# A two-block transformer kernel on one core: the blocks of the mixed branches follow the steps of the MLA's heads by a table, in place of an even spread

## What is computed

```python
proj = h @ w_in
(dn_q, dn_k, dn_v, dn_z, dn_alpha, dn_beta,
 mla_q, mla_ckv, mla_kr, gate_dn, gate_mla) = jnp.split(proj, split_at, axis=-1)
...
o_a = rms_norm(o_a, dn_norm_w) * jax.nn.silu(dn_z)          # gated output of the delta rule
y_a = o_a.reshape(B, S, DN_V) @ w_out_dn
o_b = mla_attention(mla_q, mla_ckv, mla_kr, positions, ...)   # 8 heads, 128 + 64 (rotary) columns
y_b = o_b.reshape(B, S, MLA_VD) @ w_out_mla
mix = jax.nn.sigmoid(gate_dn) * y_a + jax.nn.sigmoid(gate_mla) * y_b
x = x + gate1 * (mix @ w_o)
```

## Time and profile before

| what | value |
|---|---|
| median of 3 runs | 2372.3 us (2370.41 to 2372.65) |
| the profiled execution, time | 2371.21 us |
| its span, first to last instruction | 2369.4 us |
| mean granted TensorE clock | 0.985 of full speed |
| instructions | 26883 |
| busy: PE, DVE, ACT, POOL | 2289.3, 1117.2, 939.0, 685.2 us |
| MLA's norms and heads | about 517 to 834 |
| banded attention, gated linear attention | about 1563 to 1739, 1739 to 1845 |

### The profile page before, as it was taken

The page is one execution under the profiler, slowest core; times in us unless marked ns, Lnnn a source line. Parts: engine busy times, 40 slices in busy tenths (PEclk is TensorE's granted clock), DMA queues, the critical chain, the costliest instruction groups (busy, mean ns, idle before and its releaser), DMA issues.

```text
span 2369.4 us, 26883 instructions
## 1 busy us (share of the span) xinstructions
PE 2289.3 (97%) x10944; PEld 1857.3 (78%) x10944; DVE 1117.2 (47%) x1609; ACT 939.0 (40%) x1365; POOL 685.2 (29%) x401
## 2 busy tenths in 40 slices
PE   7899999999999999999999999999989999999998
PEld 6688889876667777888887788778767787888876
DVE  5778664435433345544311879523443252332334
ACT  4756442234443344433322242435543343332334
POOL 1243324002111253322222322321332353332334
PEclk8999999999999999999999999999999999999999
DMA  8523111211222243443333423232221432333332
GB/s 283 151 80 107 45 36 54 58 37 54 58 58 72 63 132 118 133 125 116 94 98 94 136 88 95 76 87 89 72 63 54 133 90 81 108 96 98 100 101 94
DMA packets 347983, 220.65 MB, mean 93 GB/s; under 512 B 18393, under 2 KB 327244, under 8 KB 347860
## 3 DMA queue, kind: packets, MB, share of 16 engines
q1 hardware_dynamic: 338462, 202.31, 29.0%
q10 hardware_dynamic: 9398, 16.62, 2.1%
HBM read 210.49 MB, written 8.41 MB: 92 GB/s over the span
## 4 chain that ended last, share of the span: by engine, by line
PE 87%; DVE 6%; ACT 4%; issue 1%; POOL 1%; DMA 1%; ACTq 0%; SPq 0%; DVEq 0%
PE ps L343 86%; DVE arena L372 2%; PE ps L346 1%; ACT arena L361 1%; DVE arena L364 1%; ACT scr L361 1%; DVE scr L372 1%; ACT whi L361 1%; ACT L352 0%; DVE arena L375 0%; POOL hlo L364 0%; DVE arena L368 0%; DVE arena L369 0%; DMA arena<-in_x_dram 0%; ACT L361 0%
## 5 line engine op out<-in xcount | busy, mean ns | idle before, releaser
L364 POOL TENSOR_TENSOR wlo<-wraw,whi 128x1024 fp32r<-128x1024 f32 (+1 forms) x163 | 393.5, 2414 | 1106.5 <-ACT whi L361 1106.3
L361 ACT ACTIVATE whi<-wraw 128x1024 fp32r<-128x1024 f32 (+1 forms) x328 | 341.0, 1041 | 327.6 <-PE ps L343 275.5
L343 PE MATMUL ps<-hhi,whi 128*128 128x512 f32 x1664 | 443.0, 406 | 19.9 <-ACT hhi L361 9.2
L343 PE MATMUL ps<-hhi,wlo 128*128 128x512 f32 x1664 | 420.5, 392 | 3.5 <-POOL wlo L364 3.5
L343 PE MATMUL ps<-hlo,whi 128*128 128x512 f32 x1664 | 419.3, 391 | 1.3 <-POOL hlo L364 1.2
L343 PEld LDWEIGHTS ps<-hhi,whi 128*128 128x128 f32 x1664 | 312.1, 192 | 101.3 <-issue 25.1
L343 PEld LDWEIGHTS ps<-hhi,wlo 128*128 128x128 f32 x1664 | 314.3, 189 | 70.4 <-POOL wlo L364 4.6
L343 PEld LDWEIGHTS ps<-hlo,whi 128*128 128x128 f32 x1664 | 313.8, 189 | 69.1 <-POOL hlo L364 2.1
L364 DVE TENSOR_TENSOR wlo<-wraw,whi 128x1024 fp32r<-128x1024 f32 (+2 forms) x165 | 215.4, 1305 | 295.5 <-ACT whi L361 295.3
L343 PE MATMUL ps<-arena 128*128 128x128 f32 (+6 forms) x2304 | 326.4, 295 | 12.1 <-ACT arena L361 9.6
L343 PEld LDWEIGHTS ps<-arena 128*128 128x128 f32 (+1 forms) x2304 | 277.5, 192 | 41.0 <-issue 18.8
(11 more groups left out here) (197 smaller groups left out, 2551.1 us busy)
## 6 DMA issues: line engine op xcount, KB each, us to landing
wraw<-in_w_in_dram SPq DMA_DIRECT2D x99, 512.0 KB, 3.8
wraw<-in_w_ff_dram SPq DMA_DIRECT2D x64, 512.0 KB, 3.9
wraw<-in_ffn_w_up_dram SPq DMA_DIRECT2D x44, 512.0 KB, 3.9
wraw<-in_w_gate_dram SPq DMA_DIRECT2D x32, 512.0 KB, 3.5
arena<-in_w_ada_dram SPq DMA_DIRECT2D x20, 512.0 KB, 3.9
arena<-in_w_ada_dram SPq DMA_DIRECT2D x8, 1024.0 KB, 11.4
wraw<-in_ffn_w_down_dram SPq DMA_DIRECT2D x16, 512.0 KB, 3.6
wraw<-in_w_branch_dram SPq DMA_DIRECT2D x16, 512.0 KB, 3.4
```

Of the source, the lines that this page charges most:

```text
L343: return pe.e.matmul(o, l, r, start=start, stop=stop)
L361: return ac.e.activation(o, i, f, bias=bias, scale=scale, **kw)
L364: return q.e.tensor_tensor(o, a, b, op)
```

## The change

A function `turns` takes a string of digits: after each step of the main line it advances the side line as many times as the digit says, and at the end it runs what is left. Three such strings take the place of the three even spreads.

```diff
+def turns(main, side, table):
+    for count in table:
+        next(main, None)
+        for _ in range(int(count)):
+            next(side, None)
+    run(main, side)
...
+        SIDE_MLA = '010011011200110300000100110101002101013101101101013'
+        SIDE_BAND = '0101101101101101101101101101101101'
+        SIDE_GLA = '2323323323'
...
-            weave(f.norms_then(), side, 46, 30)
+            turns(f.norms_then(), side, SIDE_MLA)
...
-            weave(f.att_pairs(), chain(f.linear("ga", f.ev_ga), f.linear("gk", f.ev_gk), f.linear("gq", f.ev_gq),
-                                       f.linear("gr", f.ev_gr), f.merge(3)), 32, 21)
+            turns(f.att_pairs(), chain(f.linear("ga", f.ev_ga), f.linear("gk", f.ev_gk), f.linear("gq", f.ev_gq),
+                                       f.linear("gr", f.ev_gr), f.merge(3)), SIDE_BAND)
...
-            weave(f.merge(2), f.gla(), 9, 24)
+            turns(f.merge(2), f.gla(), SIDE_GLA)
```

## The result

The kernel after took 2358.8 us (median of 4 runs, 2357.69 to 2362.2) against 2371.66 for the kernel before in the same session (2370.41 to 2372.65): ratio 0.9949, 95% interval 0.9936 to 0.9961. The same kernel in a second session took 2360.31, ratio 0.996 (0.9946 to 0.9975), so that about 10 to 13 us are gained and not 7. That second median would have been inside the range, by 0.3 us.

A forecast was written before the change was run, and what follows sets the result against it. PE, busy for 97% of the span, was taken as the bound, leaving only its waits and lower-clock stretches to win. Terms summed to -7.4 us, 2371.2 to 2363.8, median 2364.9, stated as 2364.5; 8-in-10 range 2360 to 2371.5.

The forecast's parts named there:

- s00 to gd.0: From first scores to the next block's high pass: 12.07 us becomes 9.8, minus 2.3, bounds zero gain and minus 4.3.
- gd.0 itself, the clock: Block behind the first scores: 7.06 us at granted clock 0.57 becomes 5.90 at full clock, minus 1.2.
- t21 with t20's lost cover: Heads 2 and 3: a block covers the 2.09 us wait at o21, minus 2.1; t20 uncovered, plus 0.5.
- t22: Heads 2 and 3, from o22 through gm.1: 12.18 us becomes 8.14, less 0.5 for the uncovered copy, net minus 3.5.
- z1.0: Mixed-branch block moved behind two uk loads: new wait of 1.6 us for its weights, bounds 0 and 4.9.
- The rival nearest in number: More gain: no wait at z1.0 and none ahead of gd.0, 3.6 us more, 2361; chance 0.11.
- the clock's rival: Both new waits, 1.6 and 2.0 us, are followed by lower-clock stretches, 2.6 us together: 2367.1; chance 0.12.
- Place one: First scores: SiLU gating moved ahead of s00 shortens the stretch to gd.0, minus 2.3, and restores the clock, minus 1.2.
- Place three: At t22, both sigmoid steps leave and blocks move, ending late high and low weight halves: net minus 3.5 us.
- The uncovered copies: Copies at t02, t20, t22 and t42 without a covering block cost 0.5 us each.
- the rival at 2.1 each: Uncovered copies at t02, t20, t22, t42 cost 2.1 us each, plus 6.4: 2370.9, no change; chance 0.16.
- The raw buffers: Rival: three weight buffers run dry at the z blocks, waits 14.6 us in place of 1.6: 2377.5, slower; chance 0.07.

The follow-up runs named there:

- gm2_ahead: Kernel after with first sigmoids and gm.0 at t22, gm.1 at o22, no block between s33 and t22, gm.2 right behind o23: 2363.80 us, ratio 0.9966.
- gating_at_t00: Kernel after with t01, t20, t41 covered, z1.0 back in its old place, gating behind the copies of t00 and t10: 2354.69 us, ratio 0.9937.
- early_only: Kernel before with only the first 11 digits of the new MLA table, the new order up to s00: 2367.90 us, ratio 0.9994.
- t21_uncovered: Kernel after with the block between t21 and o21 moved to behind s33: 2364.00 us, ratio 0.9973.
- late_only: Kernel before with the new MLA order only behind t01, the old order up to there: 2363.83 us, ratio 0.9974.
- gating_only_first: Kernel after with z1.0 to z1.3 back in their old places, the gating still ahead of s00: 2363.52 us, ratio 0.9971.
- sigmoids_back: Kernel after with both sigmoid steps back at t22 and o22, gm.0 and gm.1 with them, block behind s33 kept: 2361.42 us, ratio 0.9956.
- t22_as_before: Kernel after with no block between s33 and t22 and both sigmoid steps back at t22 and o22, gm.2 behind t40: 2361.89 us, ratio 0.9967.
- cover_only: Kernel after with one block moved to each of t01, t20 and t41, gating left ahead of s00: 2357.77 us, ratio 0.9956.

## Why the prediction was right in direction and too small in size

Term by term, forecast beside what the profile after shows in place of it. Here the remainders of the table are used where a term has no row of its own.

| step of the prediction | forecast | measured |
|---|---|---|
| s00 to gd.0 | -2.3 | -2.73 (12.07 to 9.34) |
| gd.0 itself, the clock | -1.2 | -1.53 (7.06 to 5.53) |
| t02 | -0.2 | -0.47 |
| t21 with t20's lost cover | -1.6 | -2.0 (31.27 to 29.27, before to gm2_ahead) |
| t22 | -3.5 | -3.45 (29.27 to 25.82, gm2_ahead to after) |
| t42 | -0.2 | -0.54 |
| z1.0 | +1.6 | +0.76 |
| split of the output sooner | 0 (up to 0.4, not in the sum) | -0.37 |
| sum | -7.4 | -10.33 |

- **What failed** is the size of the sum, in two of its terms above all. The largest error is z1.0, costed at +1.6 and measured at +0.76. From start to start PE was there as forecast (560.42 + 0.86 + 3.03 = 564.31, 3.9 behind the end of uv1), and z1.0 started 1.26 later, at 565.57; SP had issued the load 0.20 us after the end of uv1 and not 0.6. The other 0.5 is what the working left out: before, z1.0 started within the modelled end of the f32 group in front of it and took 5.90, and behind its wait it takes 5.57, and z1.1, no longer behind uk, takes 5.86 in place of 6.06; what is left up to s00 cancels. So part of the wait only fills what that overlap had given; the profile's own idle time, counted from the modelled end, is 0.69. The second error is the unit, and it has the same source: I took every block for 5.90 us, from that one in the earlier trace rows, while those taken off a measured stretch stand behind transposes or small products and take 5.44 to 5.57. That understates what is gained where a block is taken off a measured stretch: 0.3 at gd.0, 0.4 at t22 (where other small errors cancelled it). The rest are 0.3 to 0.4 each at s00, t02, t21, t42 and yb, left out or rounded on the cautious side. Seven errors of one sign make 2.9 us. The rival nearest in number, 2361 with neither new wait, was not what happened either: both waits came, smaller than forecast: 1.26 and 1.14 us from start to start (0.69 and 0.90 of idle time) in place of 1.6 and 2.0. For the second, gating_at_t00 shows the distance from s00 to gd.0 with no wait, 8.20 us where the prediction had about 7.8:

```profile
590.19 0.80 PE L351 MATMUL ps<-arena 128*128 128x128 f32 x4
...
598.39 2.08 PE L351 MATMUL ps<-hhi,whi 128*128 128x512 f32 x8
```

- **From sum to median.** The profiled execution moved by 9.0 in the span and by 9.0 in its time (2371.21 to 2362.2, the slowest of the four after). The first median is 3.4 below that, the second 1.9: the median of a few runs of this kernel moved by 1.5 us, which the range did not leave room for at its lower end. Of the 5.7 us between 2364.5 and 2358.8 the stretch explains 2.5 (10.33 against 7.4 and the 0.4 for the split); the other 3.2 are scatter of the medians and of what stands ahead of the stretch, so that it was also bad luck that the time fell outside the range.
- **The clock.** Forecast was 1.00 from 600 to 740, and so it is, with no wait over 0.9. But the reason was wrong: the reading that a wait of 2 us leaves the clock alone does not hold (early_only, t21_uncovered, late_only, where gd.0 waited 2.58 and its first group took 3.75 us). It rested on one wait, which was not even the longest for ACT: of the three over 2 us in the earlier trace rows, those of 2.59 and 2.63 were followed by the lower level. Of the three profiles with the 2.1 us wait at o21 two show the drop, so with waits of 1.6 and 2.0 us the clock's rival deserved more than 0.12. By the Trainium skill (TensorE: Matmul & The Clock Gate, What's actually happening) the gate knows two levels and nothing between; the trace agrees as far as stretches of 4 us tell, with 0.50 and 1.00 in full ones and values such as 0.57 or 0.70 where it changed within.
- **Place one** held as worked out: products, table load, exponentials, high half, each within 0.5 us of its estimate. What the prediction costed at zero, "POOL gets the rope steps 7 us earlier" (5.5 us in the profiles), is what makes it work: without it heads 0 and 1 take 3.6 us more (gating_only_first).
- **Place three** held in its mechanism and in its size. Not seen was which part of the edit removes it. The sigmoids' new place is worth 0.6 us (sigmoids_back); the high and low half that stood behind them went because gm.2 passed behind uk6 in the order of the weights, and that is worth 3.2 with the sigmoids in front of them (t22_as_before to gm2_ahead). The prediction named both links of the chain, sigmoids and half, and took the first for the one that the edit removes.
- **The uncovered copies** cost 0.4 to 0.8 each (cover_only covers one more in each pair of heads: minus 0.44, 0.78 and 0.51), near the 0.5 taken, and the rival at 2.1 each did not come.
- **The added table loads** show: ACT's busy time went from 939.0 to 942.1 us, 2.6 of it for two loads of 1.28. By the Trainium skill (ScalarE: Activation LUTs, What ACT_TABLE_LOAD costs) a switch costs 2.66 us with its drain; the trace again has 1.28 and the next ACTIVATE at its end, 599.66, so the measurement decides for 1.28, and both lie under blocks.
- **The raw buffers** did not run dry: z1.0 had the only wait of the z blocks. The bands and the GLA moved nothing: from yb's first product to the end both profiles take 1535.3 us.

## What to carry to other kernels

When fixed streams are interleaved, ask for each piece that PE waits for what stands ahead of it on its engine, and list the look-ahead work too: one of the costly items here (3.2 us) was a weight split that a step triggers two blocks ahead, and it moved with the order of weights that don't even need one. Put slow and independent work of ACT (table switches, long activations) right behind the copies that PE wants next and under a block of PE, not ahead of them. And a bound for a wait should carry the clock that may follow it: a wait of about 2 us cost 2 us in one profile and 5 to 6 in others.

## What the runs showed of the hardware that was not expected

- After the same 2.09 us wait of PE the granted clock was 1.00 in one profile and 0.50 in another (3.0 us more). After 1.77 us at o00, with short products behind it, it stayed near 0.5 for some 10 us.
- Over all 15 profiles, 11 waits of 1.76 to 2.74 us stand between 530 and 830. Ten were followed by a mean granted clock of 0.50 to 0.76 in the next 4 us, one (o21 before) by 1.00. Waits of up to 0.93 us, with no longer wait right behind them, left it at 1.00, and so did the wait of 1.58 or 1.59 ahead of yb, behind dense blocks, in all 15:

```profile
825.10 1.17 PE L351 MATMUL ps<-ob,whi 128*128 128x512 f32 x4 [1.58 <-ACT ob L369]
```

```profile
825.00:829.00 4.00, 3.90 (x17) 3.21 (x18) 3.65 (x3) 3.98 (x8) 3.45 (x3) 1.00 0.00 0
```

- DVE beside POOL: the four gating products took 4.06 us with POOL at work and 2.73 alone. DVE's four products for the rotations took 5.20 us beside POOL (at 586.76 in gating_only_first), and four products of the same shape 2.60 with POOL idle (at 685.95 in t22_as_before). No run varied POOL's work alone, so that POOL is the cause is argued from the times at which it worked.
